# Storing gate scratch by value group in a hybrid decoder step with product-key experts

## The reference

```python
q = (xb @ w_q).reshape(PEER_BLOCK, PEER_HEADS, 2, PEER_QDIM // 2)
s = einsum('bhpd,hpkd->bhpk', q, sub_keys)          # 8 heads x 2 halves x 128 keys
sv, si = top_k(s, 16)
cand = sv[:, :, 0, :, None] + sv[:, :, 1, None, :]
cv, ci = top_k(cand, 16)                            # 16 of 16384 experts per head
idx = i1 * N_KEYS + i2
gate = softmax(cv)
act = gelu(einsum('bhkd,bd->bhk', u_emb[idx], xb))
out = einsum('bhk,bhkd->bd', gate * act, v_emb[idx])
```

## Time and profile before

| | us |
|---|---|
| median of 3 runs (2042.26 to 2045.56) | 2043.56 |
| span of the profiled execution, first to last instruction | 2031.1 |
| busy: TensorE | 1929.3 |
| busy: VectorE | 1461.1 |
| busy: GpSimd | 810.6 |
| busy: ScalarE | 754.0 |

### The profile page before, as it was taken

One profiled execution on the slowest core, in us unless ns is written; L12 is line 12 of the kernel. 1 busy time (PEld: TensorE's weight loads), 2 busy tenths in 40 slices (PEclk: granted clock), 3 DMA queues, 4 the chain that ended last, 5 costly groups with the idle time before them and its releaser, 6 DMA issues.

```text
span 2031.1 us, 35532 instructions
## 1 busy us (share of the span) xinstructions
PE 1929.3 (95%) x14267; PEld 1754.1 (86%) x14267; DVE 1461.1 (72%) x2696; ACT 754.0 (37%) x953; POOL 810.6 (40%) x600
## 2 busy tenths in 40 slices
PE   8998977888999999999999999999999999999996
PEld 8998966676469999988888888888999999999995
DVE  6526564775257788878887897886787687778786
ACT  6334543442132224345445444543332232232232
POOL 8244737650023101322422331221688455555551
PEclk9999988999999999999999999999999999999998
DMA  6212210021222136777987887789999999999984
GB/s 202 64 56 65 64 40 2 9 91 52 83 87 84 43 140 216 260 267 269 365 316 280 305 327 286 276 285 380 390 340 358 348 325 347 358 323 353 357 309 145
DMA packets 179179, 450.11 MB, mean 222 GB/s; under 512 B 15728, under 2 KB 92272, under 8 KB 168816
## 3 DMA queue, kind: packets, MB, share of 16 engines
q1 hardware_dynamic: 125472, 240.77, 34.4%
q0 software_dynamic: 42496, 151.03, 20.5%
q10 hardware_dynamic: 11088, 56.63, 6.8%
HBM read 383.26 MB, written 65.07 MB: 221 GB/s over the span
## 4 chain that ended last, share of the span: by engine, by line
PE 51%; DVE 18%; DMA 17%; issue 9%; ACT 4%; POOL 2%; SPq 0%; ACTq 0%; DVEq 0%; POOLq 0%
PE bank L1935 23%; DMA rows_v<-in_pv,pick 11%; PE bank L1352 6%; PE bank L1889 5%; PE bank L1841 3%; DVE xs L2835 3%; DMA rows_v<-in_pv,gate 3%; DVE w_lo L2853 3%; PE bank L1944 2%; DMA sca<-in_pu_rows,pick 2%; PE bank L1372 1%; PE bank L1911 1%; DVE u_lo L2594 1%; DVE sca L2600 1%; DVE mixT L2835 1%
## 5 line engine op out<-in xcount | busy, mean ns | idle before, releaser
L834 POOL DMA_INDIRECT sca<-in_pu_rows,pick x128 | 174.1, 1360 | 527.1 <-DVE sdot L2600 413.0
L1935 PE MATMUL bank<-xhi,u_hi 128*128 128x448 f32 x1008 | 379.0, 376 | 1.2 <-ACT actb L1228 1.2
L2020 PE MATMUL bank<-w_hi,v_hi 128*128 128x416 f32 x1024 | 362.1, 354 | 14.5 <-DVE w_lo L2853 13.7
L1935 PE MATMUL bank<-xhi,u_lo 128*128 128x448 f32 x1008 | 368.9, 366 | 0.0
L1935 PE MATMUL bank<-xlo,u_hi 128*128 128x448 f32 x1008 | 368.0, 365 | 0.0
L2020 PE MATMUL bank<-w_lo,v_hi 128*128 128x416 f32 x1024 | 359.0, 351 | 0.0
L2020 PE MATMUL bank<-w_hi,v_lo 128*128 128x416 f32 x1024 | 359.0, 351 | 0.0
L834 POOL DMA_INDIRECT rows_v<-in_pv,pick x128 | 242.3, 1893 | 195.5 <-DVE xs L2835 134.5
L1281 ACT ACTIVATE v_hi<-v_raw 128x4096 fp32r<-128x4096 f32 x32 | 116.2, 3633 | 380.3 <-DMA v_raw<-in_pv 380.3
L2835 DVE SCALAR_TENSOR_TENSOR xs<-rows_v,sdot,xs 128x1024 f32<-128x1024 f32 x127 | 162.9, 1283 | 103.2 <-DMA rows_v<-in_pv,pick 97.3
L2020 PEld LDWEIGHTS bank<-w_hi,v_hi 128*128 128x128 f32 x1024 | 192.6, 188 | 24.0 <-DVE w_lo L2853 21.9
(11 more groups left out here) (694 smaller groups left out, 3587.1 us busy)
## 6 DMA issues: line engine op xcount, KB each, us to landing
u_raw<-in_pu SPq DMA_DIRECT2D x64, 1024.0 KB
v_raw<-in_pv SPq DMA_DIRECT2D x128, 512.0 KB
act_scratch<-actb ACTq DMA_DIRECT2D x64, 448.0 KB
wts<-act_scratch SPq DMA_DIRECT2D x32, 896.0 KB
gate_scratch<-gst ACTq DMA_DIRECT2D x13, 2048.0 KB
gring<-gate_scratch SPq DMA_DIRECT2D x32, 832.0 KB
wring<-in_w_q SPq DMA_DIRECT2D x4, 2048.0 KB, 9.0
wp_raw<-in_w_in SPq DMA_DIRECT2D x7, 1024.0 KB, 5.4
```

What stands on the lines that cost most here:

```text
L834: pool.indirect_dma_start(dst, None, rows[:, :], bass.IndirectOffsetOnAxis(at, 0)).then_inc(s_row[s % RING], 16)
L1935: ins = mm(bank[b][:, 0:DS], lhsT, rhs[:, 0:DS], **on)
L2020: ins = mm(bank[c][:, 0:VD], lhsT, rhs[q][:, e, 0:VD], **on)
```

## The change

gate_scratch gets the shape [32 groups, 128 partitions, 13 chunks, 4 blocks x 32 tokens]. Now everything that one group needs lies together for each partition, 13 x 512 bytes. The store of a chunk writes 32 pieces of 512 bytes for each partition, one for each group. The load of a group takes a contiguous stretch of a partition; it is made in two transfers, of 7 and of 6 chunks, and each raises s_grp by 16. The number of bytes, the tiles in SBUF and all arithmetic stay.

```diff
-        gate_d = nc.dram_tensor("gate_scratch", [NCH, 128, 128, GC], f32, kind="Internal").ap()
+        gate_d = nc.dram_tensor("gate_scratch", [EG, 128, GCH, GE * GC], f32, kind="Internal").ap()
+        gate_chunk = gate_d.rearrange("g p c n -> c p g n")
...
-            gate_v = gate_d[0:GCH].rearrange("c p (g e) t -> g p c (e t)", e=GE)
...
             def load_gates(q, g_src):
-                sp.dma_start(gring[q][:, 0:GCH, :, :].rearrange("p c e t -> p c (e t)"), g_src).then_inc(s_grp[q], 16)
+                for cs in (slice(0, 7), slice(7, GCH)):
+                    sp.dma_start(gring[q][:, cs, :, :].rearrange("p c e t -> p (c e t)"), g_src[:, cs, :].rearrange("p c n -> p (c n)")
+                                 ).then_inc(s_grp[q], 16)
...
-            load_gates(0, gate_v[0])
+            load_gates(0, gate_d[0])
...
-                    load_gates(q, gate_v[g].squeeze(0))
+                    load_gates(q, gate_d[g].squeeze(0))
...
-                    act.dma_start(gate_d[c], gst[:, c % 2, :, :]).then_inc(s_gst[c % 2], 16)
+                    act.dma_start(gate_chunk[c], gst[:, c % 2, :, :].rearrange("p (g e) t -> p g (e t)", e=GE)).then_inc(s_gst[c % 2], 16)
...
-                dve.wait_ge(s_grp[q], 32 * (g // 2 + 1))
+                dve.wait_ge(s_grp[q], 48 * (g // 2 + 1))
```

More of the change, by code:

```diff
@@ L618, in _ @@
             sp.wait_ge(S("row_used"), SLOTS)
-            load_gates(1, gate_v[1])
+            load_gates(1, gate_d[1])
             for q in range(2):
```

## The result

The changed kernel takes 2074.71 us (median of 4 runs, 2065.88 to 2078.2); the kernel before, run beside it, 2044.56 us (4 runs, 2042.26 to 2045.74). The ratio is 1.0156, 95% interval 1.0121 to 1.019: slower by some 30 us. In a second set it was 1.018 [1.0153, 1.0206]. The forecast was 2057 us, range 2026 to 2094.

The account below looks back on a forecast made before the run. TensorE was taken to bound the kernel, busy 1929.3 of 2031.1 us. Stores +26, reads -14 and between the stages +2 gave +14, a span of 2045 us; with 12.5 us around it 2057.5 us, 80% range 2026 to 2094.

Parts of the forecast that it names:

- The store side: Gate stage: stores of 4096 short runs hold ScalarE's next issue and make TensorE wait, +26 us over 13 stores.
- the read side: Value stage: group loads in long runs save DMA time, value rows come sooner and w_lo waits less, -14 us.
- I take two thirds of the best: Value stage: of the 21.9 us TensorE waits for w_lo, two thirds were taken as regained, -14 us.
- rival (b): Value stage: long reads gain nothing while ScalarE is still held behind the stores, 2071 us; chance 0.15.
- The hold, 5.7 us: Gate stage: ScalarE's act store issue is held behind a gate store of 4096 runs, at 1.5 ns a run.
- The stores' cost: Gate stage: ScalarE's delay behind each gate store, partly covered, costs TensorE 2.0 us a store, 13 stores, +26 us.
- +2 between the stages: From the last gate store to w_lo of group 1: later landing against a shorter load, +2 us, bounds -2 and +8.
- Where the DMA engines are busy at the store the hold is longer: Gate stage: a remark that some stores hold ScalarE longer, given no size of its own beside 2.0 us a store.
- the crowded case, 11.33 us: An issue behind a gate load in a crowded moment, used only as upper bound for a store's hold, 28 us.
- rival (c): Gate stage: ScalarE is held some 9 us, each store costs TensorE 5 us or more, 2099 us; chance 0.10.
- The sum's last step: Whole kernel: 12.5 us by the median lie around the span, added to 2045 us to give 2057.5 us.
- The marks named ahead: Signs: act store issue 5 to 6 us, about 13 TensorE waits of 1 to 3 us, w_lo interval 18.3 or less.

## Why the prediction was right, and where it was not

The direction and the mechanism were right: slower, because the act store is held behind a gate store of 4096 runs. The time lies inside the range of 2026 to 2094 us, but 18 us above the forecast and outside the forecast's own 2047 to 2070, since two terms were too small in opposite directions. The store side was short by some 30 us and the read side by some 10; that the second hid a third of the first was luck.

*The read side, -14 us; measured -22.5 and -24.7.* The step that failed is "I take two thirds of the best". The working ahead of it held. The change's queues from 1510 to 2000 us, for the bytes of the earlier trace rows:

```profile
q1 hardware_dynamic: 27326, 105.05, 55.9%
q0 software_dynamic: 20597, 71.28, 38.1%
```

105.05 MB took 59.0% of 510 us before, 300.9 us of all 16 engines, and 55.9% of 490 us now, 273.9 us. The 27.0 us less, times 16, over 45,330 packets are 9.5 ns each, where 10 had been read. (The gathers' own time stayed, 185.6 and 186.7 us of all engines, so this takes the rest of SyncE's queue as unchanged too.) 1.0 us a group was more than the 0.7 that TensorE lost, and all 21 us of the value stage came back. The few microseconds over that are not found in a stage: between the stages SyncE's hold of 2.05 us is gone, but with long runs on both sides w_lo of group 1 starts 46.6 us after the last store's issue (1376.92 to 1423.55), where it was 42.0 before (1375.20 to 1417.16). They are within the spread of the medians. The fear that longer packets would hold up the gathers was groundless: over the 28 intervals VectorE's waits for gathered rows fell from 85.6 and 27.5 us (pick, gate) to 71.5 and 20.3. By the rule in the Trainium skill, "DMA: Bandwidth & Descriptors", section "Specifications", that transfers run at line rate from 512 B on, this term would have been 0; the runs say 22 to 25 us, and rival (b) is out.

*The hold, 5.7 us; measured 4.81 to 5.49 where the store is alone.* 1.5 ns a run, read from one gate load, was close; it is 1.3 to 1.4. Its price there was near as well: at the six ordinary stores TensorE's waits for u_lo and hot_a, taken from one store to the next, are 9.3 us more than before, 1.5 a store where 2.0 was forecast (for u_lo 0.33 to 0.73 us at five of the six, where 0.8 had been worked out). Where the gathers are small, these waits are 27.9 us in all. The rule on the same page of the Trainium skill, section "Issuing engines are not separate DMA queues", that issue time is usually small beside the transfer, does not hold for such a store: 5.07 us of the first store's 7.9 us to its landing.

*The stores' cost, 2.0 us each, +26, and +2 between the stages; measured +56.8 and +59.0 together.* The step that failed is the end of its paragraph, "Where the DMA engines are busy at the store the hold is longer": it was written down and given no number. The earlier trace rows had the crowded case, 11.33 us, and it was put in the range only. Five stores met it with 7.95 to 10.35 us and waits for u_lo of 3.19 to 5.32 us each, with those for hot_a 26.0 us more than before, 5.2 a store; the last store met it with 14.57 us and 10.79 us of wait, in the stretch that had been put at +2. That is rival (c)'s mechanism and its size, at six of the thirteen. Its trigger was not quite the one named: short writes do not drain slower than short reads as such (27 ns a packet, against the 31 read), the queue drains slower beside gathers.

*What was missing altogether: the clock.* Waits for u_lo and hot_a rose from 7.4 us, the 1.2 for actb in it, to 52.4, +45.0 us; the slow matmuls add 86 x 0.17 = 14.6 us. Together 59.6 us, against 63.0 us by which w_lo of group 1 came later from the stores on. A quarter of the loss is thus the low clock behind the stalls. The prediction priced a stall at its length.

*The sum's last step.* 12.5 us around the span was no property of a run: the changed kernel's profiled execution took 2078.2 us at a span of 2076.4, 1.8 us. By the same 1.8 us the profiled execution of before took some 2033 us, a short one beside a median of 2044. As a difference to the median, +14 us, the sum still stands, and so does 2057.

The marks named ahead: an issue of 5 to 6 us (four of thirteen, two more just under 5), about 13 waits of 1 to 3 us for u_lo or hot_a (25 in all, eight of them in that range and seven above it), the interval at 18.3 or less (18.02), under 10 us for w_lo (none). "An issue of 9 us or more (then c)" was met too, at three of thirteen.

What stays open: whether the ordinary hold is the making of descriptors or a queue full of them. That it stretches with the gathers' bytes speaks for the queue's drain in the crowded case, but nothing separates the two for the ordinary one. Why the last store holds longest, 9.93 us even with small gathers, is open too. Nor was it tried why an act store 10 us behind a late gate store is held at some stores and not at others; between two runs of that kernel the held ones partly differed.

## What to carry to other kernels

When a layout moves short runs from a load to a store, count the runs of each DMA and look at what stands behind its issue on the same engine, with a price for the ordinary moment and one for the moment in which other queues are full. Then put the issue where nothing urgent stands behind it: the same layout that lost 34 us with the store ahead of u_hi gained 10 to 18 us with the store behind it. And price a TensorE stall of a few microseconds at more than its length.

## What was not expected of the hardware

- Shrinking another queue's transfers shortened an issue: with the gathers' bytes at an eighth, the longest hold among the first twelve stores fell from 10.35 to 5.22 us.
- Halving the runs at equal bytes at least halved the ordinary hold (4.81 to 5.49 us at 4096 runs, 1.69 to 2.70 at 2048).
- Behind eight stalls, seven of them over 3 us, 7 to 15 matmuls ran at 1.2 GHz, 0.37 us apart instead of 0.205, and cost 1.2 to 2.6 us each time.
- The same gate bytes took the DMA engines 9.5 ns longer per 512 B in runs of 512 B than in runs of 3 KB and 3.5 KB, if the rest of the queue took the same time.
